# Second layer's windowed attention: scores as pairs of 64-row products, logits negated, keys and values prepared for both groups ahead, the output's low part on GpSimd

## The chip, the cores and the metric

One core of one Trainium2 chip runs the whole program. The metric is the device time of one launch in microseconds, the median of several executions. TensorE is called PE here (PEld is its weight load), VectorE DVE, ScalarE ACT, GpSimd POOL; SP issues most transfers.

## What is computed

The reference runs one block with sparse attention, a convolution and a feed-forward part, then a second network of two layers on a sequence of 1024 rows of 1024 channels. The change is in the last layer, a sliding-window attention with a sink for each head:

```python
def swa_sink_mixer(h, kb, vb, pos_bias, mask, w_in, sinks, w_out):
    q, z = jnp.split(h @ w_in, 2, axis=-1)          # 16 heads of 64
    q = q * (HEAD_DIM ** -0.5)
    ...
    def block_fn(args):                              # a block of 128 queries, 256 keys
        s = jnp.einsum('bqhgd,bkhd->bhgqk', qn, kn) + pos_bias
        s = jnp.where(mn[None, None, None], s, NEG_INF)
        m = jnp.maximum(jnp.max(s, axis=-1, keepdims=True), sink)
        p = jnp.exp(s - m)
        p = p / (jnp.sum(p, axis=-1, keepdims=True) + jnp.exp(sink - m))
        return jnp.einsum('bhgqk,bkhd->bqhgd', p, vn)
    ...
    return (o * jax.nn.silu(z)) @ w_out
```

There are two key/value heads, each shared by eight query heads. Every product is made of three products of halves: each operand is split into a high part and a low part (value minus high part), and high by high, high by low and low by high are added up in PSUM.

## The kernel before

Each engine runs its own list of instructions, written out in program order; semaphores tie the lists together, and nothing is scheduled at run time. The program is a row of stages (index, scores, conv, gates, qkv, attend, branch, out, ffn, join, pool, keys, window, final), one function for each engine and stage: `pe_window`, `act_window`, `dve_window`, `pool_window` and `sp_window` are the stage of the change, and `*_keys` the one ahead of it, which makes queries, gates, keys and values, and in which PE multiplies by weights throughout.

The window stage has 32 items, numbered n: `ITEMS2` lists (j, hb, odd). j is a block of 128 query rows (two heads), hb the half of the sequence (four blocks of 128 queries, of which the first of hb 0 has only 128 keys and all others 256), and odd picks the head within j. Items 0 to 15 use the first key/value head, 16 to 31 the second. Each engine walks the same steps s, with the lags in `pipeline`: in step s

- PE makes the scores of item s (`score`: 4 blocks of 3 products), turns item s-3 (`turn`: 8 transposes to PSUM), and multiplies item s-4 by the values (`values`: 12 products for hb 0, 15 for hb 1);
- DVE finishes the sums of item s-2 (`norm`), adds the bias and takes the maximum of item s (`top`: 4 fused instructions on line L103, each with a short one that reads its accumulator, then a negation of the maxima on L82), and for every second item multiplies by the gate (`stored`, tile zs); it makes the low part of turned item s-3 (`turned_low`, tile p2l), the low part of the output (`stored_low`, tile o2l), and every fourth step the low part of the next queries (`begin`, tile q2l);
- ACT makes the high part of turned item s-3 (`turned`, p2h), of the output (`stored`, o2h), of the queries (`begin`, q2h), and then takes the exponentials of item s (`exps`);
- POOL scales the exponentials of item s-2 (`norm`).

The probabilities of item n live in the tile tmp of number n mod 4. SP loads the gates of the next output (zs) once the low part of the last has been made, and the final stage's loads wait for the last low part (`WINDOWED`).

PSUM has four pairs of banks, ps0 to ps3. `part_banks` sets one pair aside for outputs. In the other three, `take` gives a key (an item's scores or its transposed copy) a whole pair (`wide`) or the half that has been taken longest ago, and makes PE wait until the former key there is free. The scores are freed by DVE's `top`, the turned copy by `turned_low`.

The first layer's attention (`pe_logits`, tiles kp and qh) already makes its scores as pairs of 64-row products.

Of the kernel before, what the change touches and what calls it, by code (L numbers as in the profile page):

```python
# [7 lines left out]
F32 = mybir.dt.float32  # L8
FR = mybir.dt.float32r
# [5 lines left out]
NT = 8  # L15
# [129 lines left out]
class Net:  # L145
# [36 lines left out]
    def setup(self):  # L182
# [86 lines left out]
        self.KP = [m(f"k2p{i}", 8 + i, FR) for i in range(4)]  # L269
        self.VP = [m(f"v2p{i}", 12 + i, FR) for i in range(4)]  # L270
# [2330 lines left out]
    def pe_keys(self, e):  # L2601
# [11 lines left out]
        for j in range(16):  # L2613
            if j in (6, 8):
                self.pe_flip(e, "t2%d" % (j // 2 - 3), self.T2[j // 2 - 3])
            if j == 12:
                self.pe_values_pads(e, ("v2", 0), self.vt, ("vt",))
            if j >= 2:
                self.gemm(e, ("b", j), self.unit(("b", j), self.w8(Wb, 128 * j)), h)
# [38 lines left out]
    def act_keys(self, e):  # L2658
# [26 lines left out]
        for j in range(16):  # L2685
            if j in (6, 8):
                self.act_flip(e, "t2%d" % (j // 2 - 3), self.T2[j // 2 - 3])
            if j == 10:
                self.act_keys2(e, 0, [("zk2",)])
            if j == 12:  # L2690
                self.act_value_pads(e, ("v2", 0), (self.VP[0], self.VP[1], self.VP[2], self.VP[3]), 0, [("zv2",)])
# [17 lines left out]
    def act_keys2(self, e, kv, after):  # L2709
        kx = (self.kx0, self.kx1)[kv]  # L2710
        e.wait_ge(*self.at("kxt", kv))
        for event in after:
            e.wait_ge(*self.at(*event))
        for n, (sl, H) in enumerate(((slice(0, 64), self.KP[0]), (slice(64, 128), self.KP[2]))):
            e.activation(H[sl, :], kx[sl, :], ACT.Copy).then_inc(self.sig["ahi"].up(("k2hi", kv, n)), 1)

    def dve_keys2(self, e, kv):
        kx = (self.kx0, self.kx1)[kv]
        for n, (sl, H, L) in enumerate(((slice(0, 64), self.KP[0], self.KP[1]),
                                        (slice(64, 128), self.KP[2], self.KP[3]))):  # L2720
            e.wait_ge(*self.at("k2hi", kv, n))
            e.tensor_tensor(L[sl, :], kx[sl, :], H[sl, :].bitcast(F32), ALU.subtract).then_inc(
                self.sig["vlo"].up(("k2lo", kv, n)), 1)

    def dve_keys(self, e):
# [12 lines left out]
        for p, h in ((self.KP[0], 64), (self.KP[1], 64), (self.KP[2], 0), (self.KP[3], 0)):  # L2738
            ins = e.memset(p[h:h + 64, :].bitcast(F32), 0.0)
        ins.then_inc(self.sig["vec"].up(("zk2",)), 1)  # L2740
        self.dve_keys2(e, 0)
        self.dve_value_pads(e, ("v2", 0), (self.VP[0], self.VP[1], self.VP[2], self.VP[3]), 0)

    def pool_keys(self, e):
# [11 lines left out]
        for j in range(16):  # L2756
# [10 lines left out]
            if j == 10:  # L2767
                self.pool_zero_v(e, ((self.VP[0], 64), (self.VP[1], 64), (self.VP[2], 0), (self.VP[3], 0)), ("zv2",),
                                 [("xs", i) for i in range(NT)])
# [9 lines left out]
    def st2(self, n):  # L2779
        c = (n % 4) * 32  # L2780
        return [self.st[:, c + 4 * i:c + 4 * i + 4] for i in range(5)]

    def pe_window(self, e):
        def other_values(n):
            if n == 16:
                self.pe_values_pads(e, ("v2", 1), self.vt, ("vt",))

        def score(n):
            j, hb, odd = self.ITEMS2[n]
            QH, QL = self.qb[j % 2]  # L2790
            K = (self.KP[2], self.KP[3]) if odd else (self.KP[0], self.KP[1])
            p = self.take(e, ("s2", n))
            for event in (("q2hi", j), ("q2lo", j), ("k2lo", j // 4, odd)):
                e.wait_ge(*self.at(*event))
# [14 lines left out]
        def values(n):  # L2809
# [4 lines left out]
            V = (self.VP[2], self.VP[3]) if odd else (self.VP[0], self.VP[1])  # L2814
            PH, PL = self.pt2[odd]
            e.wait_ge(*self.at("p2lo", n))
            e.wait_ge(*self.at("vlo", ("v2", j // 4), 1))
            ks = (0, 2, 1, 3, -1) if hb else (0, 2, 1, 3)
            for k in ks:
                c0, c1 = max(k, 0) * 128, min(k + 2, 4) * 128  # L2820
                p0 = k * 256 + 128 if k >= 0 else 0
                sv, pc = slice((4 * hb + k) * 128, (4 * hb + k + 1) * 128), slice(p0, p0 + c1 - c0)
                ins = self.prods(e, po[:, c0:c1], (V[0][:, sv], V[1][:, sv]), (PH[:, pc], PL[:, pc]),
                                 odd == 0 and k == 0, odd == 1 and k == ks[-1])
# [3 lines left out]
        pipeline(32, [(4, other_values), (0, lambda n: score(n) if n != 16 else None), (3, turn), (4, values),  # L2828
                      (0, lambda n: score(n) if n == 16 else None)])
# [27 lines left out]
    def act_window(self, e):  # L2857
        def begin(n):
# [8 lines left out]
            else:  # L2867
                e.wait_ge(*self.at("prod", ("s2", 4 * j - 5)))
            e.activation(self.qb[j % 2][0][:, :], self.tmp[4][:, :], ACT.Copy).then_inc(self.sig["ahi"].up(("q2hi", j)), 1)

        def exps(n):
            j, hb, odd = self.ITEMS2[n]
            L = self.tmp[n % 4]
            mm, nm, sm, es, rd = self.st2(n)
            sk = self.sk[:, 2 * j + odd:2 * j + odd + 1]
            e.wait_ge(*self.at("top2", n))
            for i in range(4):
                o = i * 256 + (128 if hb == 0 and i == 0 else 0)
                e.activation(L[:, o:i * 256 + 256], L[:, o:i * 256 + 256], ACT.Exp, bias=nm[:, i:i + 1],
                             accum_out=sm[:, i:i + 1])  # L2880
            e.activation(es, nm, ACT.Exp, bias=sk).then_inc(self.sig["evac"].up(("exp2", n)), 1)
# [385 lines left out]
```

## Time and profile before

| | |
|---|---|
| median of 3 executions | 2695.19 us (2691.44 to 2696.88) |
| profiled execution, its own time | 2696.2 us |
| its span, first to last instruction | 2694.4 us |
| mean granted PE clock | 0.973 |
| busy: PE | 2528.4 us (94%) |
| busy: DVE | 1727.6 us (64%) |
| busy: ACT | 972.7 us (36%) |
| busy: POOL | 588.8 us (22%) |
| window stage: first score product | 2427.86 us from the span's start |
| window stage: last low part of the output begins | 2583.81 us |

Busy times are shares of the span over stages with different limits, so they say which engine is used most, and not what a change in one stage is worth. A row's duration contains a fixed latency that the next instruction overlaps; the pace of a stream is the distance between starts.

### The profile page before, as it was taken

The numbers are of one execution on the slowest core, as the hardware profiler recorded it, in microseconds if no ns is written. First come the engines' busy times: TensorE is split into PE (matmuls) and PEld (weight loads), VectorE is DVE, ScalarE is ACT, GpSimd is POOL, SyncE is SP. The second block draws the span as 40 slices with busy tenths as digits, with TensorE's granted clock in tenths as the row PEclk, the third lists the DMA queues.
The fourth block names the chain that finished last, engine by engine and source line by source line (L and its number), as shares of the span: only waits on it lengthen the run. The fifth ranks groups of instructions, "written<-read, shape, count | busy, mean of one in ns | idle before, by whom it ended". The sixth has DMA issues, their size and how long they took to land.

```text
span 2694.4 us, 31682 instructions
## 1 busy us (share of the span) xinstructions
PE 2528.4 (94%) x12088; PEld 2082.7 (77%) x12088; DVE 1727.6 (64%) x2928; ACT 972.7 (36%) x1717; POOL 588.8 (22%) x412
## 2 busy tenths in 40 slices
PE   5999999888899899999999999999999988998888
PEld 3778888667787678888888877888778766788877
DVE  5499999488424787787644368568676564008933
ACT  4431222477223322222311243233242244228732
POOL 2247422333443000000000120000000144324333
PEclk7999999899999899999999999999999989999999
DMA  4112233100454265654523132332264115232143
GB/s 165 44 40 63 79 101 100 38 1 9 137 186 135 77 208 173 198 177 140 219 95 109 59 106 79 102 107 82 94 257 156 47 55 165 85 102 68 47 146 102
DMA packets 260705, 293.16 MB, mean 109 GB/s; under 512 B 10856, under 2 KB 216140, under 8 KB 260556
## 3 DMA queue, kind: packets, MB, share of 16 engines
q1 hardware_dynamic: 260556, 291.14, 33.5%
q8 instruction: 98, 1.61, 0.2%
q14 instruction: 51, 0.42, 0.1%
HBM read 223.95 MB, written 66.10 MB: 108 GB/s over the span
## 4 chain that ended last, share of the span: by engine, by line
PE 63%; DVE 28%; ACT 5%; DMA 1%; issue 1%; POOL 1%; SPq 0%; DVEq 0%; ACTq 0%; POOLq 0%
PE ps L67 62%; DVE sm L100 6%; DVE m L97 6%; DVE tmp L103 2%; DVE tmp L79 2%; DVE sm L79 1%; ACT tmp L73 1%; DVE ptl L79 1%; PE ps L70 1%; DVE tmp L76 1%; DVE p2l L76 1%; ACT pth L73 1%; DVE wl L76 1%; DVE X L79 1%; DVE pwa L76 1%
## 5 line engine op out<-in xcount | busy, mean ns | idle before, releaser
L76 POOL TENSOR_TENSOR wl<-raw,wh 128x512 fp32r<-128x512 f32 (+1 forms) x224 | 293.2, 1330 | 1623.6 <-ACT wh L73 1623.5
L73 ACT ACTIVATE wh<-raw 128x512 fp32r<-128x512 f32 (+1 forms) x388 | 226.4, 621 | 257.5 <-PE ps L67 184.7
L73 ACT ACTIVATE tmp<-ps 128x512 f32<-128x512 f32 (+5 forms) x172 | 127.3, 751 | 391.3 <-PE ps L67 379.9
L67 PE MATMUL ps<-B2h,wh 128*128 128x512 f32 x616 | 245.3, 398 | 12.9 <-DVE B2l L76 6.7
L67 PE MATMUL ps<-B2l,wh 128*128 128x512 f32 x616 | 242.5, 394 | 0.0
L67 PE MATMUL ps<-B2h,wl 128*128 128x512 f32 x616 | 242.4, 393 | 0.0
L76 DVE TENSOR_TENSOR tmp<-tmp,ps 128x512 f32<-128x512 f32 x204 | 138.3, 684 | 108.5 <-PE ps L67 92.6
L67 PE MATMUL ps<-ah,wh 128*128 128x512 f32 (+1 forms) x608 | 191.8, 392 | 14.2 <-DVE xt L85 10.2
L73 ACT ACTIVATE wh<-ws 128x512 fp32r<-128x512 f32 x152 | 94.4, 627 | 289.0 <-DVE ws L76 261.9
L67 PE MATMUL ps<-B3h,wh 128*128 128x512 f32 x448 | 178.3, 398 | 15.2 <-DVE B3l L76 7.0
L67 PE MATMUL ps<-al,wh 128*128 128x512 f32 (+1 forms) x608 | 190.4, 390 | 0.0
L67 PE MATMUL ps<-ah,wl 128*128 128x512 f32 (+1 forms) x608 | 190.3, 390 | 0.0
L67 PE MATMUL ps<-B3h,wl 128*128 128x512 f32 x448 | 176.0, 393 | 0.0
L67 PE MATMUL ps<-B3l,wh 128*128 128x512 f32 x448 | 176.0, 393 | 0.0
L100 DVE MATCH_REPLACE8 sm<-m,sm 128x384 f32<-128x384 f32 (+2 forms) x192 | 166.4, 872 | 0.0
L97 DVE MAX8 m<-sm 128x8 f32<-128x384 f32 (+2 forms) x192 | 160.6, 876 | 0.0
L67 PEld LDWEIGHTS ps<-B2h,wh 128*128 128x128 f32 x616 | 117.2, 190 | 42.7 <-issue 8.0
L67 PEld LDWEIGHTS ps<-ah,wh 128*128 128x128 f32 (+1 forms) x608 | 113.5, 187 | 41.9 <-DVE xt L85 10.4
L76 DVE TENSOR_TENSOR X<-X,ps 128x1024 f32<-128x1024 f32 (+1 forms) x56 | 59.6, 1067 | 132.3 <-PE ps L67 132.3
L67 PEld LDWEIGHTS ps<-B2h,wl 128*128 128x128 f32 x616 | 117.3, 190 | 25.1
L67 PEld LDWEIGHTS ps<-B2l,wh 128*128 128x128 f32 x616 | 117.3, 190 | 24.0 <-issue 0.2
L67 PEld LDWEIGHTS ps<-ah,wl 128*128 128x128 f32 (+1 forms) x608 | 113.6, 187 | 24.9 <-issue 0.4
(281 smaller groups left out, 5806.8 us busy)
## 6 DMA issues: line engine op xcount, KB each, us to landing
ada<-in_ada_w SPq DMA_DIRECT2D x48, 512.0 KB, 3.9
raw<-in_w_in SPq DMA_DIRECT2D x37, 512.0 KB, 4.4
raw<-in_a_w_in SPq DMA_DIRECT2D x33, 512.0 KB, 4.6
gates<-tmp SPq DMA_DIRECT2D x32, 512.0 KB, 3.0
raw<-in_w_ffn_gate SPq DMA_DIRECT2D x24, 512.0 KB, 6.4
hd<-tmp SPq DMA_DIRECT2D x22, 512.0 KB, 4.5
gf<-hd SPq DMA_DIRECT2D x22, 512.0 KB, 7.2
raw<-in_a_w_out SPq DMA_DIRECT2D x20, 512.0 KB, 3.5
```

The lines of the kernel that those rows point to most:

```text
L67: return self.e.matmul(*a, **k) if self.e else Ins()
L70: return self.e.transpose(*a, **k) if self.e else Ins()
L73: return self.e.activation(*a, **k) if self.e else Ins()
L76: return self.e.tensor_tensor(*a, **k) if self.e else Ins()
L79: return self.e.scalar_tensor_tensor(*a, **k) if self.e else Ins()
L97: return self.e.max(*a, **k) if self.e else Ins()
L100: return self.e.match_replace(*a, **k) if self.e else Ins()
L103: return self.e.tensor_tensor_reduce(*a, **k) if self.e else Ins()
```

## The change

- **Scores.** The keys are no longer padded with zero rows to 128 rows for each head. Keys of a key/value head stand twice in one tile, on rows 0 to 63 and 64 to 127, and the two heads of a query block are multiplied in turn on the two halves of the rows, into two PSUM banks. `score` works in even steps alone, for items n and n+1 together, and takes four banks one by one: the first two blocks of both items go to one pair, the last two to another. `top` waits for and frees each half by itself.
- **Logits.** DVE stores the logits with their sign turned (`scale` -1, minimum in place of maximum, against the negated sinks nsk), so that ACT takes the exponential with scale -1 and the negation on L82 is gone.
- **Keys and values.** Those of both key/value heads are made ready in the stage ahead; the values stand in one tile v2c with 64 zero columns between the blocks. The work at item 16 (`other_keys`, `other_values`) is gone.
- **Low part of the output.** It moves from DVE to POOL, at the end of POOL's step.

```diff
-        self.KP = [m(f"k2p{i}", 8 + i, FR) for i in range(4)]
-        self.VP = [m(f"v2p{i}", 12 + i, FR) for i in range(4)]
+        self.K2 = [(m(f"k2h{i}", 8 + 2 * i, FR), m(f"k2l{i}", 9 + 2 * i, FR)) for i in range(2)]
+        self.vc = m("v2c", 12, FR, cols=4096)
+        self.vend = self.sb("v2e", 51, 192, FR, 2048)
+        self.nsk = self.sb("nsk", 51, 16, F32, 2816)
...
     def dve_keys2(self, e, kv):
-        kx = (self.kx0, self.kx1)[kv]
-        for n, (sl, H, L) in enumerate(((slice(0, 64), self.KP[0], self.KP[1]),
-                                        (slice(64, 128), self.KP[2], self.KP[3]))):
-            e.wait_ge(*self.at("k2hi", kv, n))
-            e.tensor_tensor(L[sl, :], kx[sl, :], H[sl, :].bitcast(F32), ALU.subtract).then_inc(
-                self.sig["vlo"].up(("k2lo", kv, n)), 1)
+        e.wait_ge(*self.at("k2hi", kv))
+        e.tensor_tensor(self.K2[kv][1][:, :], (self.kx0, self.kx1)[kv][:, :], self.K2[kv][0][:, :].bitcast(F32),
+                        ALU.subtract).then_inc(self.sig["vlo"].up(("k2lo", kv)), 1)
...
     def pe_window(self, e):
-        def other_values(n):
-            if n == 16:
-                self.pe_values_pads(e, ("v2", 1), self.vt, ("vt",))
-
         def score(n):
+
             j, hb, odd = self.ITEMS2[n]
-            QH, QL = self.qb[j % 2]
-            K = (self.KP[2], self.KP[3]) if odd else (self.KP[0], self.KP[1])
-            p = self.take(e, ("s2", n))
-            for event in (("q2hi", j), ("q2lo", j), ("k2lo", j // 4, odd)):
-                e.wait_ge(*self.at(*event))
+            if odd:
+                return
+            (QH, QL), (KH, KL) = self.qb[j % 2], self.K2[j // 4]
             for i in range(4):
+                if i % 2 == 0:
+                    ps = [self.take(e, ("s2", n + k, i // 2), False) for k in (0, 1)]
+                for event in (("q2hi", j), ("q2lo", j), ("k2lo", j // 4)):
+                    e.wait_ge(*self.at(*event))
                 blk = 4 * hb + i
                 c, k = slice(blk * 128, blk * 128 + 128), slice(max(blk - 1, 0) * 128, blk * 128 + 128)
-                o = i * 256 + (128 if blk == 0 else 0)
-                ins = self.prods(e, p[:, o:i * 256 + 256], (QH[:, c], QL[:, c]), (K[0][:, k], K[1][:, k]), True, True)
-            ins.then_inc(self.sig["prod"].up(("prod", ("s2", n))), 1)
+                o = i % 2 * 256 + (128 if blk == 0 else 0)
+                for t, (q, kk) in enumerate(((QH, KH), (QH, KL), (QL, KH))):
+                    for p, r in zip(ps, (slice(0, 64), slice(64, 128))):
+                        ins = e.matmul(p[:, o:i % 2 * 256 + 256], q[r, c], kk[r, k], start=t == 0, stop=t == 2)
+                if i % 2:
+                    ins.then_inc(self.sig["prod"].up(*(("prod", ("s2", n + k, i // 2)) for k in (0, 1))), 1)
...
-        pipeline(32, [(4, other_values), (0, lambda n: score(n) if n != 16 else None), (3, turn), (4, values),
-                      (0, lambda n: score(n) if n == 16 else None)])
+        pipeline(32, [(0, score), (3, turn), (4, values)])
...
-        def other_keys(n):
-            if n == 16:
-                self.act_keys2(e, 1, [("prod", ("s2", 15))])
-
-        def other_values(n):
-            if n == 16:
-                self.act_value_pads(e, ("v2", 1), (self.VP[0], self.VP[1], self.VP[2], self.VP[3]), 64, [("pv2", 15)])
-
-        pipeline(32, [(4, other_values), (0, other_keys), (3, turned), (5, stored), (-2, begin), (0, exps)])
+        pipeline(32, [(3, turned), (5, stored), (-2, begin), (0, exps)])
...
             for i in range(4):
-                o = i * 256 + (128 if hb == 0 and i == 0 else 0)
+                p = self.ps(("s2", n, i // 2))
+                o = 128 if hb == 0 and i == 0 else 0
+                e.wait_ge(*self.at("prod", ("s2", n, i // 2)))
                 ins = e.tensor_tensor_reduce(
-                    L[:, o:i * 256 + 256], p[:, o:i * 256 + 256],
-                    self.T2[j // 4][:, hl * 256 + o - i * 256:hl * 256 + 256], 1.0, sk, ALU.add, ALU.max, mm[:, i:i + 1])
-            ins.then_inc(vec.up(("most2", n), ("free", ("s2", n))), 1)
-            e.wait_ge(*self.at("most2", n))
-            e.tensor_scalar(nm, mm, -1.0, None, ALU.mult).then_inc(vec.up(("top2", n)), 1)
+                    L[:, i * 256 + o:i * 256 + 256], p[:, i % 2 * 256 + o:i % 2 * 256 + 256],
+                    self.T2[j // 4][:, hl * 256 + o:hl * 256 + 256], -1.0, nsk, ALU.add, ALU.min, mm[:, i:i + 1])
+                if i % 2:
+                    ins.then_inc(vec.up(("free", ("s2", n, i // 2)), *([("top2", n)] if i == 3 else [])), 1)
...
-        pipeline(32, [(4, other_values), (0, other_keys), (2, norm), (0, top), (5, stored), (3, turned_low),
-                      (5, stored_low), (-2, begin)])
+        pipeline(32, [(2, norm), (0, top), (5, stored), (3, turned_low), (-2, begin)])
...
-        pipeline(32, [(2, norm), (0, top)])
+        def stored_low(n):
+            j, hb, odd = self.ITEMS2[n]
+            if odd:
+                hs = slice(hb * 512, hb * 512 + 512)
+                e.wait_ge(*self.at("z2hi", n // 2))
+                e.tensor_tensor(self.o2l[j][:, hs], self.zs[:, :], self.o2h[j][:, hs].bitcast(F32), ALU.subtract).then_inc(
+                    self.sig["plo"].up(("z2lo", n // 2)), 1)
+
+        pipeline(32, [(2, norm), (0, top), (5, stored_low)])
```

How the lists of instructions change is seen at three places. Before, PE in step 7 ends the scores of item 7 in ps2 and turns item 4 into ps0 (s_vec is the semaphore by which DVE frees score banks, s_gps POOL's, s_vlo that of DVE's low parts):

```order
L67 MATMUL ps2<-k2p2_517,q2h1_531 128x256
L67 MATMUL ps2<-k2p3_518,q2h1_531 128x256
L67 MATMUL ps2<-k2p2_517,q2l1_532 128x256
L70 MATMUL ps0<-ident_75,tmp0_70 128x128 [waits s_gps,s_vec]
L70 MATMUL ps0<-ident_75,tmp0_70 128x128 x7
```

Here ps0 held the scores of item 6, one step back. After the change, PE in step 6 makes the scores of items 6 and 7, and turns item 3 behind them:

```order
L67 MATMUL ps0<-k2h0_515,q2h1_530 128x256 [waits s_vec]
L67 MATMUL ps0<-k2h0_515,q2h1_530 128x256
L67 MATMUL ps0<-k2l0_516,q2h1_530 128x256 x2
L67 MATMUL ps0<-k2h0_515,q2l1_531 128x256 x2
...
L67 MATMUL ps1<-k2h0_515,q2h1_530 128x256 x2
L67 MATMUL ps1<-k2l0_516,q2h1_530 128x256 x2
L67 MATMUL ps1<-k2h0_515,q2l1_531 128x256 x2
L70 MATMUL ps2<-ident_75,tmp3_73 128x128 [waits s_gps,s_vlo]
L70 MATMUL ps2<-ident_75,tmp3_73 128x128 x7
```

and in step 7, after the values of item 3, it turns item 4, again into ps0:

```order
L67 MATMUL ps3<-p2h0_524,v2c_519 128x128
L70 MATMUL ps0<-ident_75,tmp0_70 128x128 [waits s_gps,s_vec]
L70 MATMUL ps0<-ident_75,tmp0_70 128x128 x7
L67 MATMUL ps3<-p2h1_526,v2c_519 128x256 [waits s_vlo]
L67 MATMUL ps3<-p2l1_527,v2c_519 128x256
```

What moved: ps0 now holds the first halves of items 6 and 7 together. By `take`, each item with an even number n is turned into the pair of banks with the first halves of items n+2 and n+3, and each odd item into that of the item turned before it. On DVE, before, step 7 reads item 7 from ps2, and the low part of item 4 from ps0 follows its last row and a negation:

```order
L88 RECIPROCAL st_85<-st_85 128x4 [waits s_vec]
L103 ISA tmp3_73,st_85<-ps2,t20_523,sk_87 128x256 [waits s_prod]
L103 ISA st_85 128x1
...
L82 TENSOR_SCALAR st_85<-st_85 128x4 [waits s_vec]
L76 TENSOR_TENSOR p2l0_526<-ps0,p2h0_525 128x1024 [waits s_ahi]
```

and after the change:

```order
L103 ISA tmp3_73,st_85<-ps0,t20_522,nsk_521 128x256 [waits s_prod]
L103 ISA st_85 128x1
L103 ISA tmp3_73,st_85<-ps0,t20_522,nsk_521 128x256
L103 ISA st_85 128x1
L103 ISA tmp3_73,st_85<-ps1,t20_522,nsk_521 128x256
...
L76 TENSOR_TENSOR p2l0_525<-ps0,p2h0_524 128x1024 [waits s_ahi]
```

The negation is gone, and the two rows that read ps0 for item 7 stand directly ahead of two others and of the row that reads the turned item 4 from the same pair.

## Rows read from the trace of the kernel before

**Rows 1.** Windows view, us busy (instructions): by engine, PE clock, DMA share, GB/s.
```profile
2460.00:2480.00 20.00, 19.34 (x161) 18.44 (x160) 19.69 (x62) 16.50 (x49) 9.40 (x8) 1.00 0.18 54
...
2520.00:2525.00 5.00, 4.96 (x42) 4.72 (x42) 4.93 (x19) 3.02 (x11) 2.43 (x3) 1.00 0.04 10
```

**Rows 2.** The chain in order of time: start us, us, what; four of its eight q2l rows.
```profile
2471.76 1.14 DVE q2l L76
...
2488.91 1.14 DVE q2l L76
...
2511.08 1.14 DVE q2l L76
...
2531.69 1.14 DVE q2l L76
```

**Rows 3.** Groups by line, 2400 to 2694 us: busy, mean ns, idle before, releaser.
```profile
L76 POOL TENSOR_TENSOR wl<-raw,wh 128x512 fp32r<-128x512 f32 x32 | 41.4, 1317 | 67.6 <-ACT wh L73 67.6
...
L82 DVE TENSOR_SCALAR st<-st 128x4 f32<-128x4 f32 x32 | 14.4, 451 | 1.1
...
L76 DVE TENSOR_TENSOR o2l<-zs,o2h 128x512 fp32r<-128x512 f32 x16 | 10.8, 678 | 0.7 <-ACT o2h L73 0.7
```

**Rows 4.** The chain at the end of the window stage.
```profile
2575.68 1.11 PE ps L70 x8
...
2576.81 1.03 ACT p2h L73
...
2577.87 1.22 DVE p2l L76
...
2579.72 2.68 DMA zs<-qd
```

**Rows 5.** Timeline of PE's weight loads in two steps of the window stage.
```profile
2467.20 0.19 PEld L67 LDWEIGHTS ps<-p2h,v2p 128*128 128x128 f32 x1 [0.23 <-DVE p2l L76]
...
2468.94 0.30 PEld L67 LDWEIGHTS ps<-k2p,q2h 128*128 128x128 f32 x2
...
2470.38 0.90 PEld L70 LDWEIGHTS ps<-ident,tmp 128*128 128x128 f32 x8
...
2471.25 0.19 PEld L67 LDWEIGHTS ps<-p2h,v2p 128*128 128x128 f32 x1
```

**Rows 6.** Timeline of PE, products on 64 rows in the first layer.
```profile
126.55 0.41 PE L67 MATMUL ps<-kp,qh 64*128 64x256 f32 x4
...
126.78 0.29 PE L67 MATMUL ps<-kp,ql 64*128 64x256 f32 x2
...
535.34 0.28 PE L67 MATMUL ps<-kp,ql 64*128 64x256 f32 x2
...
535.55 0.44 PE L70 MATMUL ps<-ident,tmp 128*128 128x128 f32 x2
```

**Rows 7.** Timeline of DVE in one step of the window stage.
```profile
2455.65 0.15 DVE L76 TENSOR_TENSOR st<-st 128x4 f32<-128x4 f32 x1
...
2456.71 0.09 DVE L103 DVE_READ_ACCUMULATOR2_ANT st<- 128x1 f32 x1
```

**Rows 8.** Timeline of ACT and DVE around a query block.
```profile
2470.05 0.63 ACT L73 ACTIVATE o2h<-zs 128x512 fp32r<-128x512 f32 x1 [0.79 <-DVE zs L76]
...
2470.59 1.04 ACT L73 ACTIVATE q2h<-tmp 128x1024 fp32r<-128x1024 f32 x1
...
2471.68 1.22 DVE L76 TENSOR_TENSOR q2l<-tmp,q2h 128x1024 fp32r<-128x1024 f32 x1
```

**Rows 9.** PE timeline: first work after long idle stretches.
```profile
521.99 0.69 PE L67 MATMUL ps<-kp,qh 64*128 64x128 f32 x4 [3.00 <-DVE vp L76]
...
2427.86 0.66 PE L67 MATMUL ps<-k2p,q2h 128*128 128x128 f32 x2 [3.41 <-DVE q2l L76]
...
2519.14 0.38 PE L67 MATMUL ps<-p2h,v2p 128*128 128x256 f32 x1 [2.36 <-DVE v2p L76]
```

**Rows 10.** The chain's row of the first 24 score products.
```profile
2427.86 5.48 PE ps L67 x24
```

More of the change, by code:

```diff
@@ L2688, in act_keys @@
             if j == 10:
-                self.act_keys2(e, 0, [("zk2",)])
+                for i in range(NT):
+                    e.wait_ge(*self.at("xs", i))
+                for kv in (0, 1):
+                    self.act_keys2(e, kv)
             if j == 12:
-                self.act_value_pads(e, ("v2", 0), (self.VP[0], self.VP[1], self.VP[2], self.VP[3]), 0, [("zv2",)])
+                e.wait_ge(*self.at("zv2"))
+                e.wait_ge(*self.at("prod", "v2t"))
+                for kv in (0, 1):
+                    for hi, of in self.v2_blocks(kv, 0):
+                        e.activation(hi, of(self.ps("v2t")), ACT.Copy).then_inc(self.sig["ahi"].up(("v2hi", kv)), 1)
             if j >= 2:
@@ L2707, in act_keys, with act_keys2, v2, v2_parts @@
                 e.activation(self.tmp[i % 5][:, :], self.ps(("b", j)), ACT.Silu).then_inc(done, 1)
-    def act_keys2(self, e, kv, after):
-        kx = (self.kx0, self.kx1)[kv]
+    def act_keys2(self, e, kv):
         e.wait_ge(*self.at("kxt", kv))
-        for event in after:
-            e.wait_ge(*self.at(*event))
-        for n, (sl, H) in enumerate(((slice(0, 64), self.KP[0]), (slice(64, 128), self.KP[2]))):
-            e.activation(H[sl, :], kx[sl, :], ACT.Copy).then_inc(self.sig["ahi"].up(("k2hi", kv, n)), 1)
+        e.activation(self.K2[kv][0][:, :], (self.kx0, self.kx1)[kv][:, :], ACT.Copy).then_inc(
+            self.sig["ahi"].up(("k2hi", kv)), 1)
     def dve_keys2(self, e, kv):
-        kx = (self.kx0, self.kx1)[kv]
-        for n, (sl, H, L) in enumerate(((slice(0, 64), self.KP[0], self.KP[1]),
-                                        (slice(64, 128), self.KP[2], self.KP[3]))):
-            e.wait_ge(*self.at("k2hi", kv, n))
-            e.tensor_tensor(L[sl, :], kx[sl, :], H[sl, :].bitcast(F32), ALU.subtract).then_inc(
-                self.sig["vlo"].up(("k2lo", kv, n)), 1)
+        e.wait_ge(*self.at("k2hi", kv))
+        e.tensor_tensor(self.K2[kv][1][:, :], (self.kx0, self.kx1)[kv][:, :], self.K2[kv][0][:, :].bitcast(F32),
+                        ALU.subtract).then_inc(self.sig["vlo"].up(("k2lo", kv)), 1)
+    def v2(self, kv, low, blk, odd):
+        m = 16 * kv + 8 * low + blk
+        if m == 31:
+            return self.vend[:, 64 - 64 * odd:192 - 64 * odd]
+        return self.vc[:, 128 * m + 64 - 64 * odd:128 * m + 192 - 64 * odd]
+    def v2_parts(self, kv):
+        rows = lambda p: p.rearrange("p (i c) -> p i c", c=128)
+        c, n = 2048 * kv, 7 if kv else 8
+        yield rows(self.vc[:, c:c + 128 * n])[:, :, 64:128], None
+        if kv:
+            yield self.vc[:, c + 960:c + 1024], None
+    def v2_blocks(self, kv, low):
+        c = 2048 * kv + 1024 * low
+        n = 7 if kv and low else 8
+        rows = lambda p: p.rearrange("p (i c) -> p i c", c=128)
+        yield rows(self.vc[:, c:c + 128 * n])[:, :, 64:128], lambda p: rows(p[:, 0:128 * n])[:, :, 64 * kv:64 * kv + 64]
+        if n == 7:
+            yield self.vend[:, 64:128], lambda p: p[:, 896 + 64 * kv:960 + 64 * kv]
     def dve_keys(self, e):
@@ L2873, in exps @@
             L = self.tmp[n % 4]
[L2874 removed]
+            mm, sm, es, rd = self.st2(n)
             sk = self.sk[:, 2 * j + odd:2 * j + odd + 1]
```

66 lines of the change are left out of this document (29 added, 37 removed).

## The prediction, as it stood before the run

> **What bounds the kernel now.** The change touches the window stage and a little of the stage ahead, where PE multiplies by weights throughout and DVE and ACT have room; so I read the window stage. The windows view comes first: in a stretch from its middle DVE is busy 19.69 of 20 us, PE 19.34 and ACT 16.50, at full clock [rows 1]. PE's busy time contains latency that its neighbours overlap, so this alone doesn't say who leads. The chain does: it runs on DVE, and the row that comes once in four items (q2l) repeats after 17.15 us, twice after more: 22.17 and 20.61 us around item 16, where keys and values of the second group are made [rows 2]. DVE sets the pace, 17.15 us for four items, and the two long rounds cost 5.02 + 3.46 = 8.48 us. Four items take eight rounds; the tail behind them waits for the gate's load and the last low parts [rows 4].
>
> **What the change takes from the engines.** DVE loses four negations a round, 451 ns each, and two low parts of the output, 678 ns each: 1.80 + 1.36 us [rows 3]. That leaves 17.15 - 3.16 = 14.0 us. ACT keeps its work: 16.50 of 20 us is 14.15 us a round [rows 1]. On PE the first layer shows the new form of scores: four 64-row products of 256 columns start 0.23 us ahead of the next two, so a pair takes 0.115 us [rows 6]. A 128-row product takes as long: 15 products of values take 1.74 us, 0.116 each [rows 5]. So PE's scores fall from 2.78 to 1.38 us for two items. A change of mode costs about 0.10 us: two products start 0.21 us ahead of the transposes behind them, where one pair needs 0.115 [rows 6]. POOL gets a low part of 1.32 us for every two items [rows 3] and is busy 9.40 of 20 us [rows 1], so it has room.
>
> If that were all, a round would fall to 14.15 us. But PSUM sets another order. Of three pairs of banks, scores of two items now hold two at once. An even item n is turned into the pair that holds the first halves of items n+2 and n+3, so its transposes wait until DVE has read the first half of item n+3, in the same step in which DVE wants the result. Before, they waited for item n+2, read a step earlier. The Trainium skill warns of this in "TensorEngine Tiling (Array Packing)", section Restrictions and Gotchas: row tiling raises PSUM pressure, since different row tiles write to different banks. It gives no figure for it; by the rows it is what the next part works out, and by the same page's section Theoretical Speedup (up to 2 times for 64 rows) alone, PE's scores would just halve, as [rows 6] show, and the first rival below would hold.
>
> I follow one cycle, from DVE's reading of an odd item's first half to the same of the next pair:
> 1. PE gets the signal, 0.04 us (the gap between two links of the chain is 0.02 to 0.04 [rows 4]), and turns the even item: 0.87 us until the next load [rows 5].
> 2. PE multiplies an earlier item's values: 1.74 us for hb 1, 12 products or 1.39 us for hb 0.
> 3. Mode change, 12 pairs of scores, mode change: 0.10 + 1.38 + 0.10 us.
> 4. PE turns the odd item, ACT makes its high part, DVE starts on its low part: 2577.87 - 2575.68 = 2.19 us [rows 4].
> 5. DVE's low part takes 1.13 us (1.22, the next starting 0.09 before its end). In every second cycle q2l follows, and it needs q2h, which now no low part of the output covers: from o2h to q2l are 1.63 us, and o2h starts 0.1 us ahead of p2l, so q2l starts 1.53 us behind p2l and takes 1.13 [rows 8].
> 6. From the sums of the next item to the end of its first half: 1.15 us [rows 7], 0.15 less when the first block has 128 keys.
>
> Long cycle (q2l; values of hb 0): 0.04 + 0.87 + 1.39 + 1.58 + 2.19 + 1.53 + 1.13 + 1.15 = 9.88 us. Short cycle: 0.04 + 0.87 + 1.74 + 1.58 + 2.19 + 1.13 + 1.00 = 8.55 us. A round is 18.43 us, 1.28 more than before. DVE's other work fits between: the even item's low part starts 2.2 us after the signal and the next top ends near 5.8 us, ahead of the odd item's low part at 6.2. ACT's exponentials too.
>
> **The sum**, against the profiled execution's 2696.2 us (1.0 above the median of 2695.19):
> - Rounds from item 7 to 31: 6 x 18.43 = 110.6 against 6 x 17.15 + 8.48 = 111.4: -0.8 us. What the second group's preparation gives back, the longer rounds take. It moves into the stage ahead, where PE covers it; without that cover it would cost up to the 8.48 again.
> - The start: the first top waits for 6 pairs instead of 12 products, at the lower clock, where 24 products took 5.48 us, 0.228 each [rows 10]. A pair there I take at 0.25: 1.5 instead of 2.7 us. Bounds 0 and -3; I take -1.5.
> - The end: the last low part, on the path to the final stage's loads, takes 1.32 instead of 0.68 us, and the wait for the banks comes once more. Bounds 0.6 and 2; I take +1.2.
> - At full clock that makes 2695.1 us, no change.
> - The clock. In a long cycle PE works 0.87 + 1.39 + 1.58 + 0.87 + 1.74 = 6.45 us, and with 0.2 us of latency stands idle some 3.2 us; in a short one 1.9. Two rows show what follows on such an idle time: after 3.00 us four products of 128 columns took 0.69 us, more than the 0.41 of four twice as wide [rows 9, 6], and after 3.41 us 24 products took 5.48 us where 24 x 0.116 = 2.78 would do [rows 10]. That is the lower of two levels, 1.2 against 2.4 GHz. After 2.36 us the clock was still at 1.00 [rows 9, 1]. Since PE's work is on the path right behind the idle time (4 us of it), a fall costs up to 5.48 - 2.78 = 2.70 us. Seven cycles are long. Bounds: none falls, 0; all fall and the short ones now and then, 7 x 2.7 + 7 = 26 us. I take four to five falls: +12.
>
> So **2707 us**.
>
> **Rivals.**
> - *The ring of banks doesn't bind.* Then the shorter scores and DVE's lost work both reach the time [rows 3, 6], and the floor is ACT's: 6 x 14.15 = 84.9 instead of 111.4, -26.5, so with start and end 2669 us. For it: DVE leads now and loses 3.16 us a round. Against it: the order of the instructions, in which an even item's transposes stand behind a semaphore of the same step's top. It decides if the turned item comes back within the 0.8 us of the second half's reading; transposes and high part alone take 2.19. Chance 0.12.
> - *The ring binds, but the clock holds:* 2695 us, within 5.4 us of before. For it: idle times of 2.36 us left the clock alone [rows 1, 9]. Chance 0.25, of which 0.04 lie below the bound of 0.2%, by a better start.
> - *A cheaper ring:* PE or DVE picks up half of the lost round (steps 3 and 5 shorter): 2696 - 8 = 2688 us. Chance 0.05.
> - *More than I sum:* half-rate PE stretches the short cycles as well, 2720 us and more. Chance 0.08.
> - My forecast, between 2700 and 2720: 0.50.
>
> **The numbers.** 0.2% is 5.4 us, about what a measurement of this kernel can tell from no change. Slower: 0.50 + 0.08 = 0.58; faster: 0.12 + 0.04 + 0.05 = 0.21; the same: 0.21. The range must leave out at most 2 in 10: the ring that doesn't bind lies below, the worst of the clock above, so 2687 to 2721. My forecast's own range is 2700 to 2720.
>
> **What the profile after should show.** Rounds of q2l of 18.4 us at full clock and more with falls, none of them long at item 16. DVE idle ahead of every second p2l, about 1.4 us, released by ACT's p2h, and behind it PE's transposes released by DVE's L103: that is the ring. No L82 on the chain, pairs of 64x256 at 0.115 us, idle stretches of PE of 3 us followed by products at the lower level. The forecast is wrong if transposes of even items don't wait for DVE, if DVE is busy above 95% in the middle of the stage, or if the clock stays at 1.00 with idle stretches of 3 us.

## The result, and the profile after

| | before | after |
|---|---|---|
| median | 2694.36 us (2691.44 to 2696.88, 4 runs) | 2729.06 us (2728.75 to 2730.21, 4 runs) |
| span of the profiled execution | 2694.4 us | 2727.4 us |
| mean granted clock over the span | 0.973 | 0.962 |

The changed kernel is slower: ratio 1.0125, 95% interval 1.0113 to 1.0137. Forecast were 2707 us and 2687 to 2721, so the direction is right and the size is outside the range. The runs below say which terms were too small.

The windows view of the kernel after. Before, DVE was busy 19.69 of 20 us at full clock in the same place [rows 1]:

```profile
core 0: us, PE busy (x) PEld busy (x) DVE busy (x) ACT busy (x) POOL busy (x), PEclk, DMA share, GB/s
2460.00:2480.00 20.00, 15.74 (x127) 14.99 (x126) 12.99 (x37) 13.20 (x38) 8.52 (x7) 0.83 0.05 16
2480.00:2500.00 20.00, 15.68 (x118) 15.05 (x119) 12.27 (x42) 11.10 (x38) 8.29 (x7) 0.74 0.18 53
2500.00:2520.00 20.00, 13.96 (x94) 13.40 (x93) 12.86 (x40) 11.40 (x33) 9.01 (x7) 0.74 0.15 50
...
2580.00:2600.00 20.00, 15.10 (x137) 14.47 (x136) 14.95 (x47) 14.34 (x46) 10.41 (x8) 0.92 0.08 28
```

No engine is full any more, and the granted clock is 0.74 to 0.92. So neither an engine nor the clock alone sets the pace; a chain of waits does. The waits view from 2430 to 2600 us names its links:

```profile
engine line waited for: us in total, times, longest us
...
ACT p2h L73 <- PE ps L70: 60.6, 28, 4.6
...
PE ps L70 <- DVE st L103: 40.5, 14, 3.5
DVE p2l L76 <- ACT p2h L73: 38.2, 28, 2.3
```

TensorE's transposes wait 14 times, once for each even item from 2 to 28, for DVE's L103, the maxima. That is the ring of banks of the prediction. The timeline of TensorE shows what stands behind those waits (start, duration; in brackets the idle time before and its releaser):

```profile
2481.78 1.94 PE L70 MATMUL ps<-ident,tmp 128*128 128x128 f32 x8 [3.49 <-DVE st L103]
...
2489.60 1.70 PE L70 MATMUL ps<-ident,tmp 128*128 128x128 f32 x8
...
2495.20 1.06 PE L70 MATMUL ps<-ident,tmp 128*128 128x128 f32 x8 [2.55 <-DVE st L103]
...
2499.18 1.09 PE L70 MATMUL ps<-ident,tmp 128*128 128x128 f32 x8
...
2505.46 1.94 PE L70 MATMUL ps<-ident,tmp 128*128 128x128 f32 x8 [3.49 <-DVE st L103]
```

Eight transposes take 1.06 us at full clock and 1.94 at the lower level. Read the starts of the turns with brackets: from 2481.78 to 2495.20, a short cycle after an idle of 3.49 us, 13.42 us; from 2495.20 to 2505.46, a long cycle at full clock, 10.26. (The prediction calls a cycle long when it holds q2l.) The short cycle is the longer one here, since both turns and all products between them run at the lower level. Of the six idles of 3.49 us in the stage, five were followed by a turn of 1.94 us and one was not:

```profile
2578.19 1.06 PE L70 MATMUL ps<-ident,tmp 128*128 128x128 f32 x8 [3.49 <-DVE st L103]
```

DVE's rows of q2l, the round of four items, are 23.5 and 23.7 us apart, where [rows 2] have 17.15:

```profile
2455.62 1.45 DVE L76 TENSOR_TENSOR q2l<-tmp,q2h 128x1024 fp32r<-128x1024 f32 x1 [0.23 <-ACT q2h L73]
...
2479.15 1.45 DVE L76 TENSOR_TENSOR q2l<-tmp,q2h 128x1024 fp32r<-128x1024 f32 x1 [0.24 <-ACT q2h L73]
...
2502.84 1.45 DVE L76 TENSOR_TENSOR q2l<-tmp,q2h 128x1024 fp32r<-128x1024 f32 x1 [0.23 <-ACT q2h L73]
```

They show something that the prediction did not have: 1.45 us, where the same instruction took 1.22 [rows 8]. The sum of 128x4 ahead of every reciprocal grew too, in every fourth item. DVE's timeline and, in the last row, GpSimd's:

```profile
2584.67 1.23 DVE L76 TENSOR_TENSOR p2l<-ps,p2h 128x1024 fp32r<-128x1024 f32 x1 [0.51 <-ACT p2h L73]
2585.81 0.70 DVE L76 TENSOR_TENSOR st<-st 128x4 f32<-128x4 f32 x1
```

```profile
2585.23 1.27 POOL L76 TENSOR_TENSOR o2l<-zs,o2h 128x512 fp32r<-128x512 f32 x1 [1.25 <-ACT o2h L73]
```

A sum of four columns takes 0.70 us and ends at 2586.51; GpSimd's low part of the output ends at 2586.50. p2l, which reads PSUM and one tile in SBUF, overlaps the same instruction and keeps its 1.23 us.

So there were four suspects: the ring of banks, the clock that falls in its idles, the meeting of DVE and GpSimd, and TensorE's 64-row products. The base of every comparison below is 2729.06 us; the kernel before took 2695.5 to 2697.0 us (medians) beside these runs.

### The profile page after: what moved, and what is told of

It reads as the page before. It is cut to its first block, busy times and chain, and to the rows that moved or that the text cites. A ratio compares the mean times of both kernels' runs of the same rounds, so it can differ in the third digit from the quotient of the medians.

```text
span 2727.4 us, 31644 instructions
## 1 busy us (share of the span) xinstructions
PE 2527.8 (93%) x12080; PEld 2083.5 (76%) x12080; DVE 1708.7 (63%) x2874; ACT 970.0 (36%) x1713; POOL 609.9 (22%) x426
## 3 DMA queue, kind: packets, MB, share of 16 engines
q8 instruction: 98, 1.61, 0.2%
## 4 chain that ended last, share of the span: by engine, by line
PE 66%; DVE 25%; ACT 5%; DMA 1%; issue 1%; POOL 1%; SPq 0%; DVEq 0%; ACTq 0%; POOLq 0%
PE ps L67 63%; DVE sm L100 6%; DVE m L97 6%; PE ps L70 3%; DVE tmp L79 2%; DVE sm L79 1%; ACT tmp L73 1%; DVE ptl L79 1%; DVE tmp L76 1%; ACT pth L73 1%; DVE tmp L103 1%; ACT p2h L73 1%; DVE X L79 1%; DVE pwa L76 1%; DVE wl L76 1%
## 5 line engine op out<-in xcount | busy, mean ns | idle before, releaser
L100 DVE MATCH_REPLACE8 sm<-m,sm 128x384 f32<-128x384 f32 (+2 forms) x192 | 175.1, 964 | 0.0
L97 DVE MAX8 m<-sm 128x8 f32<-128x384 f32 (+2 forms) x192 | 169.3, 967 | 0.0
```

Of the source, the lines that this page charges most:

```text
L97: return self.e.max(*a, **k) if self.e else Ins()
L100: return self.e.match_replace(*a, **k) if self.e else Ins()
```

## Experiments

The expectations say row, or row of scores, for what is called an item here.

### The clock: e3_fill_idle and e11_fill_half

Zero weights in products that add to the open sum of values fill the idle time ahead of the even turns. Nothing else is moved; e11_fill_half has 5 of them in place of 10.

```diff
         def turn(n):
+            if n >= 2 and n % 2 == 0:
+                for i in range(10):
+                    e.matmul(self.ps(("o2", n // 2 - 1))[0:64, :], self.vend[:, 0:64], self.pt2[0][0][:, 0:512],
+                             start=False, stop=False)
             p, L = self.take(e, ("p2", n)), self.tmp[n % 4]
```

> The changed kernel with ten products of 512 columns with zero weights ahead of each even row's turn, put into the idle time in which TensorE waits for the bank (they add zero to the open sum of the values). Nothing else is moved. Theory A (21 us of the loss is the clock that falls in those idles of 2.5 to 3.5 us): the granted clock of the window rises from 0.74 to 0.83 to above 0.95 and the kernel takes 2729 - 21 = about 2708 us (2704 to 2714). Theory B (the clock falls by the shape of the products, or its level is not on the path): 2729 us, or a few us more where the added products end after the bank comes free.

Measured: 2703.66 us (2700.37 to 2706.35), ratio to before 1.0029 [1.002, 1.0039]. Theory A holds, with 25.4 us in place of 21. From 2460 us on the windows view has full clock, and q2l comes every 19.6 us (2472.28 and 2491.90):

```profile
2480.00:2500.00 20.00, 18.48 (x159) 15.63 (x158) 15.80 (x50) 14.49 (x44) 10.86 (x9) 1.00 0.16 53
```

> e3_fill_idle with five products of zeros in place of ten, so that TensorE's idles ahead of the even turns are cut from 3.5 and 2.5 us to some 2.4 and 1.4 us. Theory A (idles of that length leave the clock alone, as one of 2.36 us did in the kernel before): full clock, rounds of 19.6 us, about 2703 us, as with ten. Theory B (they don't): clock between 0.75 and 0.95 and 2710 to 2725 us.

Measured: 2710.36 us (2706.01 to 2712.3), clock 0.86 to 1.00 by windows. That is theory B, at its near end; a shorter idle is better and not safe. Three turns behind the same idle time:

```profile
2455.56 1.56 PE L70 MATMUL ps<-ident,tmp 128*128 128x128 f32 x8 [2.36 <-DVE st L103]
...
2476.72 1.94 PE L70 MATMUL ps<-ident,tmp 128*128 128x128 f32 x8 [2.36 <-DVE st L103]
...
2497.76 1.07 PE L70 MATMUL ps<-ident,tmp 128*128 128x128 f32 x8 [2.37 <-DVE st L103]
```

One keeps the clock, one loses it and one loses it in part. From 2455 to 2559 us there are six such idles; behind two the turn took 1.06 and 1.07 us, behind the other four 1.56 to 1.94. So the length of the idle alone does not say whether the clock falls. That the idles matter and not the 64-row products is shown by two runs: e3_fill_idle has as many of these products and full clock, and e7_single_rows below, which has nothing added, runs them one at a time without idle time and has 1.00 in every window from 2460 to 2540 us.

### The ring at full clock, step by step

e3_fill_idle shows the ring without the clock. A short cycle on TensorE (the turn of the even item, first product of values, first of scores, turn of the odd item, next even turn):

```profile
2474.94 1.06 PE L70 MATMUL ps<-ident,tmp 128*128 128x128 f32 x8 [1.23 <-DVE st L103]
2475.76 0.36 PE L67 MATMUL ps<-p2h,v2c 128*128 128x256 f32 x1
...
2477.63 0.33 PE L67 MATMUL ps<-k2h,q2h 64*128 64x128 f32 x2
...
2479.23 1.09 PE L70 MATMUL ps<-ident,tmp 128*128 128x128 f32 x8
...
2484.27 1.06 PE L70 MATMUL ps<-ident,tmp 128*128 128x128 f32 x8 [0.29 <-DVE st L103]
```

and on DVE, which continues it (p2l, the sum, the reading of the first half's second maximum):

```profile
2481.42 1.23 DVE L76 TENSOR_TENSOR p2l<-ps,p2h 128x1024 fp32r<-128x1024 f32 x1 [0.51 <-ACT p2h L73]
2482.56 0.74 DVE L76 TENSOR_TENSOR st<-st 128x4 f32<-128x4 f32 x1
...
2484.08 0.09 DVE L103 DVE_READ_ACCUMULATOR2_ANT st<- 128x1 f32 x1
```

Differences of these starts against the prediction's steps, and the same for the long cycle that follows:

| step | short, measured (forecast) | long, measured (forecast) |
|---|---|---|
| signal and even turn | 0.10 + 0.82 (0.04 + 0.87) | 0.09 + 0.82 (0.04 + 0.87) |
| values, change of mode | 1.87 (1.84) | 1.54 (1.49) |
| scores, change of mode | 1.60 (1.48) | 1.61 (1.48) |
| odd turn to p2l | 2.19 (2.19) | 2.19 (2.19) |
| p2l; in the long cycle then q2l | 1.14 (1.13) | 1.47 + 1.41 (1.53 + 1.13) |
| sum to the end of the first half | 1.61 (1.00) | 1.15 (1.15) |
| cycle | 9.33 (8.55) | 10.28 (9.88) |

Of 1.18 us that a round is longer than forecast, 0.89 lie in two places, 0.61 from the sum on and 0.28 at q2l: both are instructions of DVE with both sources in SBUF, beside GpSimd's low part.

### DVE and GpSimd: e1_low_on_dve and e5_fill_low_dve

```diff
-        pipeline(32, [(2, norm), (0, top), (5, stored), (3, turned_low), (-2, begin)])
+        pipeline(32, [(2, norm), (0, top), (5, stored), (3, turned_low), (5, stored_low), (-2, begin)])
...
-        pipeline(32, [(2, norm), (0, top), (5, stored_low)])
+        pipeline(32, [(2, norm), (0, top)])
```

> The changed kernel with the output's low part (o2l) back on DVE, everything else as changed. Theory A (DVE's instructions with both sources in SBUF wait while GpSimd's subtraction runs; that costs the ring 0.23 us at q2l and 0.55 us at the 128x4 sum, 4.7 us in all): q2l comes back from 1.45 to 1.22 us and the sums to 0.15 us, while 12 o2l of 0.68 us join the ring of banks (+8.2 us): 2729 - 4.7 + 8.2 = about 2732.5 us. Theory B (the long q2l and sums have another cause, such as the new tiles): they stay at 1.45 and 0.63, and the time is 2729 + 8.2 = about 2737 us.

Measured: 2726.6 us (2725.72 to 2732.72), below both numbers. The durations are theory A's: q2l 1218 ns, sums 154 ns on average (291 in the kernel after, same stretch). The time is neither's; the granted clock was 0.85 and 0.92 in its first two windows from 2440 us, where the changed kernel had 0.76 and 0.83. With the clock free to move, the time does not tell the two apart. So the same edit was made on e3_fill_idle:

> e3_fill_idle (the products with zero weights, which hold the clock) with the output's low part back on DVE. At full clock e3_fill_idle has rounds of 19.62 us, a long cycle of 10.28 and a short one of 9.33. Theory A (DVE waits for GpSimd's subtraction): q2l loses 0.27 us and the sums of the short cycle 0.59, the idle 0.24 us ahead of q2l goes too, and two o2l of 0.68 us (0.59 between starts) join: 10.28 - 0.27 - 0.24 + 0.59 = 10.36 and 9.33 - 0.59 + 0.59 = 9.33, rounds of 19.7 us, 2704 us, no change. Theory B (no such wait): 10.28 - 0.24 + 0.59 = 10.63 and 9.33 + 0.59 = 9.92, rounds of 20.55 us, 2703.7 + 6 x 0.93 = about 2709 us.

Measured: 2702.55 us (2698.9 to 2705.58), e3_fill_idle 2703.66; q2l at 2472.04, 2491.67 and 2511.30, rounds of 19.63 us. Theory A gave 19.7, theory B 20.55. DVE's groups from 2460 to 2540 us, out of the lines view:

```profile
L76 DVE TENSOR_TENSOR o2l<-zs,o2h 128x512 fp32r<-128x512 f32 x8 | 5.5, 682 | 0.0
L76 DVE TENSOR_TENSOR q2l<-tmp,q2h 128x1024 fp32r<-128x1024 f32 x4 | 4.9, 1220 | 0.0
...
L76 DVE TENSOR_TENSOR st<-st 128x4 f32<-128x4 f32 x16 | 2.5, 155 | 0.0
```

Per round, DVE had given away two o2l of 0.60 us between starts, 1.20 us. Moving them cost it 0.59 at the sum, 0.27 at q2l and 0.24 of idle ahead of q2l, 1.10 us: nearly all, and the round agrees (19.62 with o2l on GpSimd, 19.63 with it on DVE). The page "SBUF — State Buffer" of the Trainium skill, section Who interferes with whom, has this rule: a DVE instruction with two SBUF inputs contends with a GpSimd instruction that reads SBUF, for a pair of ports that is an exclusive lock; with at most one SBUF input, and outside DVE's two-port modes, it does not contend. The rows of q2l, the sum and p2l agree with it.

The kernel before has a row that the number of inputs alone does not explain, a negation with one source, in SBUF:

```profile
2469.06 0.37 DVE L82 TENSOR_SCALAR st<-st 128x4 f32<-128x4 f32 x1
```

```profile
2467.51 1.89 POOL L76 TENSOR_TENSOR tmp<-tmp,st 128x1024 f32<-128x1024 f32 x1 [1.37 <-DVE st L88]
```

It ends at 2469.43, GpSimd's scaling at 2469.40. Of the 32 L82, 28 began beside a scaling; 15 of them ended 0.01 to 0.04 us after it, and 13 ended 0.02 to 0.03 us after the zeroing (L91) behind it. The other four took 0.17 us. Whether the L82 ran in a two-port mode, which the rule leaves out, no run shows.

### The ring: e2_wide_banks, e4_wide_low_dve, e7_single_rows

Each row of scores gets both banks of one tile, and the two rows of a pair two tiles, in place of half a tile each of both.

```diff
-                if i % 2 == 0:
-                    ps = [self.take(e, ("s2", n + k, i // 2), False) for k in (0, 1)]
+                if i == 0:
+                    ps = [self.take(e, ("s2", n + k)) for k in (0, 1)]
...
-                        ins = e.matmul(p[:, o:i % 2 * 256 + 256], q[r, c], kk[r, k], start=t == 0, stop=t == 2)
+                        ins = e.matmul(p[:, o:i * 256 + 256], q[r, c], kk[r, k], start=t == 0, stop=t == 2)
```

DVE's reads follow, and it frees an item's tile once, after its fourth block, in place of two halves.

> The changed kernel with the scores' PSUM banks taken wide: each row of scores has one tile of two banks for itself, where now the two rows of a pair share both tiles by halves. An even row's turn then waits for the maxima of the even row, which end one step earlier, not for the first half of the odd row's maxima. Theory A (the loss is the ring of banks plus the clock that falls in its idles): TensorE's idles of 2.5 to 3.5 us ahead of the even turns go, the clock stays near full, a round of four rows takes 15 to 16.5 us in place of 23, and the kernel 2729 - 6 x (23.05 - 16) = about 2687 us (2680 to 2695). Theory B (the clock is low since products of 64 rows do not hold it): granted clock stays near 0.75 to 0.83, rounds near 20, about 2712 us. Theory C (another wait takes the place at once, the turn of the odd row for the low part before it): rounds of 18, about 2700 us.

Measured: 2680.97 us (2680.51 to 2683.94), ratio to before 0.9947 [0.9931, 0.9964], 48 us below the changed kernel: theory A, and 6 us better than its number. No engine's work differs, only where the scores land and so which maxima a turn waits for. The windows view, and TensorE's wait for DVE out of the waits view from 2460 to 2540 us:

```profile
2500.00:2520.00 20.00, 17.56 (x170) 16.74 (x169) 18.70 (x56) 17.80 (x50) 13.00 (x10) 1.00 0.17 54
```

```profile
PE ps L67 <- DVE st L103: 9.3, 9, 1.6
```

No even turn waits 2.5 us any more; now the scores wait for the odd item's maxima, 1.6 us at most. q2l comes 16.06 us apart at full clock and 16.9 to 17.6 where it dips. The dips come three times, behind three of the six idles of 1.62 to 1.68 us that TensorE has ahead of the scores from 2456 to 2541 us, so an idle much shorter than 3 us can be followed by the lower level too. The profiled execution was the slowest of the four (2683.94 us); the others took 2680.5 to 2681.2.

> As e2_wide_banks, and the output's low part back on DVE. If DVE sets the pace once the ring is gone, the 16 subtractions of 0.68 us cost what GpSimd's waits no longer do: 16 x 0.68 - 16 x 0.78 / 2 = about 4.6 us more than e2_wide_banks. If ACT or TensorE sets it, the two are within 1.5 us of each other.

Measured: 2684.69 us (2681.07 to 2688.06). The medians are 3.7 us apart, nearer to the 4.6 than to the 1.5, but the ranges overlap, and at full clock its rounds are 16.13 us against 16.06: no difference that can be told.

e7_single_rows takes the pairs away and keeps the 64-row keys:

```diff
-            if odd:
-                return
+            r, p = slice(64 * odd, 64 * odd + 64), self.take(e, ("s2", n))
...
-                    for p, r in zip(ps, (slice(0, 64), slice(64, 128))):
-                        ins = e.matmul(p[:, o:i * 256 + 256], q[r, c], kk[r, k], start=t == 0, stop=t == 2)
+                    ins = e.matmul(p[:, o:i * 256 + 256], q[r, c], kk[r, k], start=t == 0, stop=t == 2)
```

> e2_wide_banks with the scores of one row at a time, in its own step: 12 products of 64 rows for each item, and no second row beside them. So TensorE spends 12 x 0.116 = 1.4 us more for two items, and an even row's turn waits for nothing new. Theory A (the pairs themselves bring little, what counts is which maxima a turn waits for, and DVE's lighter work): rounds of 16 to 16.5 us where e2_wide_banks has 16.06, 2681 to 2686 us. Theory B (TensorE's saved time is the gain): rounds of 17.5, 2681 + 6 x 1.4 = about 2690 us or more.

Measured: 2683.9 us (2683.35 to 2685.51), rounds of 16.62 us, a little above theory A's 16 to 16.5. Theory A on the time. TensorE is full:

```profile
2480.00:2500.00 20.00, 20.00 (x163) 19.05 (x163) 18.76 (x59) 16.93 (x53) 12.34 (x9) 1.00 0.17 54
```

At full clock the pairs are worth 16.62 - 16.06 = 0.56 us a round. Over the stage that does not arrive: five rounds of q2l took 83.10 us here (2451.99 to 2535.09) and 83.57 in e2_wide_banks, whose clock dips, and both profiled executions took 2684.0 us. The medians differ by 2.9 us and the ranges just meet. So the gain of the pairs is 3 us at most, and not shown.

### One part of the change alone: e6_before_neg

In this diff `sk` is taken from the negated sinks, as in the change.

```diff
-                    self.T2[j // 4][:, hl * 256 + o - i * 256:hl * 256 + 256], 1.0, sk, ALU.add, ALU.max, mm[:, i:i + 1])
+                    self.T2[j // 4][:, hl * 256 + o - i * 256:hl * 256 + 256], -1.0, sk, ALU.add, ALU.min, mm[:, i:i + 1])
...
-            e.tensor_scalar(nm, mm, -1.0, None, ALU.mult).then_inc(vec.up(("top2", n)), 1)
...
-            e.activation(es, nm, ACT.Exp, bias=sk).then_inc(self.sig["evac"].up(("exp2", n)), 1)
+            e.activation(es, mm, ACT.Exp, bias=sk).then_inc(self.sig["evac"].up(("exp2", n)), 1)
```

> The kernel before with one part of the change alone: the logits negated, so that the maxima come out negated and DVE's 32 negations of 451 ns (L82) go. Scores, banks, keys, values and low parts are as before. Theory A (DVE alone sets the pace before): 32 x 0.45 = 14.4 us less, about 2681 us. Theory B (TensorE, busy 19.34 of 20 us, is close behind and takes over): a round falls from 17.15 to about 16, 8 x 1.1 = 9 us less, about 2687 us. Theory C (the chain of banks sets it and the negation lay in its shade): 2695 us.

Measured: 2687.53 us (2685.14 to 2688.91), ratio 0.9963 [0.9949, 0.9977]. Theory B: q2l at 2452.49, 2468.12 and 2483.76, rounds of 15.64 us where before had 17.15, with TensorE busy 20.00 of 20 us. The two rounds around item 16 still take 22.24 and 19.04 us. This edit was a gain of 9.5 us by itself, and the change buried it.

Two things follow that no run tested. The two long rounds are 10.0 us above 2 x 15.64. Preparing the second group's keys and values ahead as the change does, but keeping the padded 128-row scores, would by this estimate give 2687.5 - 10.0, about 2677.5 us, less than any run here; it holds if the stage ahead covers that work (the window stage's first q2l starts at 2426.49 us before and at 2426.53 after). And e7_single_rows, with TensorE just as full, has rounds 0.98 us longer than this kernel. Its 64-row scores need eight changes of mode a round; 0.98 / 8 = 0.12 us each, an estimate, is near the 0.10 that the prediction read. So no run shows that the 64-row form itself pays.

### Three tries to go below e2_wide_banks

e8_wide_turn_first: `pipeline(32, [(3, turn), (0, score), (4, values)])` on TensorE.

> e2_wide_banks with TensorE's order changed in even steps: the turn of the odd row comes ahead of the scores of the next pair, not behind them, and so fills the idle time of 0.7 to 1.6 us in which the scores wait for the odd row's maxima (DVE L103). Theory A (that chain, maxima, scores, turn, high part, low part, maxima, sets the round of 16.06 us): the scores' 1.6 us leave it, DVE's work of 15.0 us becomes the round, 6 us less, about 2675 us. Theory B (the scores then come 1.4 us later and DVE waits for them where it now waits for nothing; a wait takes the other's place): each of 14 cycles gets 0.5 to 0.8 us longer, about 2690 us.

Measured: 2698.1 us (2694.13 to 2700.73). Theory B, and more than it gave: rounds of 18.6 us. A second wait came that I had not listed, for the bank that p2l frees (waits view, 2460 to 2540 us):

```profile
DVE tmp L103 <- PE ps L67: 12.2, 10, 1.6
...
PE ps L70 <- DVE p2l L76: 9.9, 9, 1.3
```

e10_low_later: `(6, stored_low)` for `(5, stored_low)` on GpSimd.

> e2_wide_banks with GpSimd's low part of the output one step later in its order, behind the scaling of the next row, so that it no longer runs beside q2l and beside the sum of the odd row. Theory A (only what waits on the chain costs): the chain loses 0.59 us in the short cycle and 0.27 in the long one, 6 x 0.86 = 5 us, about 2676 us. Theory B (the wait moves: another sum or the next scaling on GpSimd meets it, and that is on the chain as well): within 1.5 us of 2681, or longer.

Measured: 2699.05 us (2695.7 to 2703.21), rounds of 18.0 to 18.8 us. q2l is back at 1.23 us, so the meeting is avoided there; the sum still meets it once a round and takes 0.54 to 0.55 us. The gate's load into zs waits for that low part, takes 2.7 to 2.9 us, and now ends last (same view):

```profile
DVE zs L76 <- DMA zs<-qd: 10.3, 9, 1.6
```

Theory B in its result and in the sum that is met after all, but most of the 18 us come by a wait of neither theory's. Avoiding a short wait on one engine made a load late.

e9_wide_fill: three products of zeros of 512 columns ahead of the last product of values of each odd row.

> e2_wide_banks with three products of 512 columns with zero weights put among the odd row's values, 0.65 us of work in the 0.7 to 1.6 us that TensorE stands idle ahead of the next scores. Theory A (e2_wide_banks loses some 4 to 5 us to the clock: its rounds take 17.49, 16.95 and 16.88 us at the start and one 17.61 later, where those at full clock take 16.06): rounds of 16.1 us throughout, about 2676 us. Theory B (those rounds are long for another reason, or the added work comes on the chain): 2681 us or 2 to 3 us more.

Measured: 2681.95 us (2678.79 to 2682.79). In the profiled execution theory A's rounds are there, 16.05 to 16.08 us from 2451.82 to 2532.15, five of them in 80.33 us, where e2_wide_banks took 83.57. The medians, 0.98 us apart with overlapping ranges, don't show the 3 us. The traces compare extremes: the profiled execution is the fastest of four here and was the slowest of four there. Unclear.

## Why the prediction was too low

The sum had two parts, 2695.1 us at full clock and 12 for the clock. e3_fill_idle separates them: 2703.7 at full clock and 25.4 for the clock, together 2729.1. So 8.6 us of the miss are in the first and 13.4 in the second. (The filling products may cost a little themselves at the two ends of the stage, where the turn at 2445.07 and those from 2571.84 on follow them without a wait.)

- **What GpSimd's part costs DVE** was put at nothing: this step failed. The prediction takes two low parts of the output, 1.36 us a round, off DVE and says of POOL that "it has room". That is true of the work and false of the time. In the sum of the ring, step 5 has 1.13 us for q2l and step 6 has 1.00 us up to the end of the first half; they measured 1.41 and 1.61, so 0.28 + 0.61 = 0.89 us a round. The evidence stood in the trace of before, in the L82 shown above: the mean of 451 ns [rows 3] is mostly waiting for GpSimd, where the 128x4 sum took 0.15. I took it as the price of a negation.
- **The ring** was right in place and order: the 14 waits of L70 for L103, DVE's idle ahead of each second p2l (1.45 us at full clock, forecast 1.4), no L82, no round of e3_fill_idle longer at item 16 than its neighbours. Step 3 (scores) came to 1.60 instead of 1.48, 0.25 us a round. With the first point a round at full clock is 19.62 instead of 18.43, 6 x 1.19 = 7.1 us; the other 1.5 of the 8.6 are left for the start and the end.
- **The clock** was the right mechanism with a wrong price: the term of +12 us measured 25.4. The number of falls was nearly right, five behind the six idles of 3.49 us, where I took four to five. What failed is the 2.70 us for a fall. It was read from [rows 10], where the products ran at the lower level for 5.3 us (2427.9 to about 2433.2). Here they ran at it from 2481.78 to about 2491, 9.2 us, over the whole of the short cycle's path on TensorE, and behind that comes the cycle's own idle of 2.55 us (1.9 in the prediction). Six short cycles took 72.4 us in place of 6 x 9.33 = 56.0, so 16.4 us, 2.7 each on average but over 4 in the three where the level stayed low longest (13.42, 13.53, 13.58); the long ones add some 5. My upper bound, 7 x 2.7 + 7 = 26 us, held, but by luck: its price for a fall was too low and its number of falls too high; the value that I took did not.
- **The row that misled**: after an idle of 2.36 us the clock was still at 1.00 [rows 9, 1]. One row is one case; e11_fill_half has six idles of that length, and four of them cost clock.
- **The rivals.** "The ring doesn't bind" (2669) fell: it binds, and removing it by wider banks gives 2681, not 2669, since another chain (maxima, scores, turn, high part, low part) then sets 16.06 us (its links follow each other without a gap in e2_wide_banks' trace), where I had ACT's 14.15. "The clock holds" (2695) fell at 2703.7 even when it was made to hold. "More than I sum", with half-rate PE in the short cycles as well, to which I gave 0.08, is what happened. None of the three signs by which the forecast would have been wrong appeared: they tested the mechanism, and what failed were prices.

What stays open: the start and the end of the stage were not tried by themselves, and neither were e2_wide_banks and e9_wide_fill measured often enough to tell them apart.

## What to carry to other kernels

When an edit makes work for two items at once, write down which tile each half of the output lands in and whose release the next user waits for, one step on. Here splitting each tile between two rows turned a gain of 15 us (e2_wide_banks against before) into a loss of 35, of which 25 is clock, with the same instructions. And price a fall of the clock over the work up to the next idle time, not up to the end of the first burst. Moving work to an idle engine has to be priced with what it makes the other one wait. And measure the parts of a change alone: here the negation was worth 9.5 us and the pairs 3 at most.

## What the runs showed of the hardware

- An instruction of DVE with both sources in SBUF that meets a GpSimd subtraction which reads SBUF is held up to its end: a sum of 128x4 took 0.74 us in place of 0.15 and ended 0.01 to 0.02 us after it; q2l took 1.45 to 1.48 in place of 1.22. With one source in PSUM p2l kept its 1.23 us. A negation of 128x4 with its one source in SBUF was held too, 0.31 to 0.65 us in place of 0.17 (kernel before).
- After six idles of TensorE of 2.36 and 2.37 us in one execution (e11_fill_half) the clock stayed up twice (transposes of 1.06 and 1.07 us) and was at the lower level for all or part of the turn four times (1.56 to 1.94 us). After six of 3.49 us (changed kernel) it was at the lower level five times, once until about 9.2 us of work later.
- Behind three of six idles of 1.62 to 1.68 us (e2_wide_banks) the clock fell some 0.4 to 1.6 us into the work that followed: turns of 1.97, 1.92 and 1.77 us.
- 64-row products do not lower the clock by themselves: one at a time and without idle time it stayed at 1.00 from 2460 to 2540 us (e7_single_rows).
- A pair of 64-row products of 256 columns takes 0.118 us (e3_fill_idle: 12 pairs with both changes of mode 1.60 to 1.61 us), as long as one 128-row product (0.116 us [rows 5]).
